# Attention's suffix sums: low parts of the later key chunks added by GpSimd, then multiplied by ones once

## The reference

```python
z = einsum('bqhd,bkhd->bhqk', q, k) * HEAD_DIM ** -0.5 + bias
causal = k_pos[None, :] < q_pos[:, None]
log_1m = where(causal, log_sigmoid(-z), 0.0)              # = -softplus(z)
suffix = cumsum(log_1m, axis=3, reverse=True) - log_1m    # over all later keys
att = where(causal, exp(log_sigmoid(z) + suffix), 0.0)
out = einsum('bhqk,bkhd->bqhd', att, v)
```

## Time and profile before

| what | value |
|---|---|
| median of 3 runs | 1523.05 us |
| the profiled execution | 1527.67 us, its span 1526.1 us |
| TensorE busy | 1472.7 us, 97% of the span |
| VectorE busy | 979.4 us, 64% |
| ScalarE busy | 911.1 us, 60% |
| GpSimd busy | 256.0 us, 17% |
| attention, from the first high part to the last `turn_scores` | 860.0 to 1023.7 |
| HBM traffic | 271.65 MB, 178 GB/s over the span |

### The profile page before, as it was taken

How to read it: one execution, slowest core, us unless ns; L and a number is a source line. 1 busy time by engine, 2 the same in 40 slices (tenths; PEclk the granted TensorE clock), 3 DMA queues, 4 the chain that set the end, 5 groups by cost and what they waited for, 6 DMA issues and landing times.

```text
span 1526.1 us, 28437 instructions
## 1 busy us (share of the span) xinstructions
PE 1472.7 (97%) x11288; PEld 1355.4 (89%) x11288; DVE 979.4 (64%) x1486; ACT 911.1 (60%) x1660; POOL 256.0 (17%) x446
## 2 busy tenths in 40 slices
PE   5999989999999999999999989999999999999998
PEld 3887659999999999999889956678999999999997
DVE  4799965797644887644536346654797654776743
ACT  4699876776643776534435556654776644666633
POOL 1389800000000232100000021110000000222200
PEclk9999999999999999999999999999999999999999
DMA  9887682255554455643337366653255554455553
GB/s 363 310 300 263 264 279 93 69 166 167 176 181 151 141 167 166 196 164 132 127 115 260 106 217 231 222 194 104 68 166 167 166 190 156 138 178 164 190 170 100
DMA packets 71765, 273.76 MB, mean 179 GB/s; under 512 B 8032, under 2 KB 10096, under 8 KB 71120
## 3 DMA queue, kind: packets, MB, share of 16 engines
q1 hardware_dynamic: 65248, 246.44, 47.5%
q0 software_dynamic: 6096, 25.15, 4.9%
q10 hardware_dynamic: 288, 0.35, 0.1%
HBM read 262.80 MB, written 8.85 MB: 178 GB/s over the span
## 4 chain that ended last, share of the span: by engine, by line
PE 84%; DVE 7%; ACT 4%; issue 2%; DMA 1%; SPq 0%; DVEq 0%; ACTq 0%
PE ps L704 62%; PE ps L681 6%; PE ps L937 4%; PE ps L754 2%; DVE w_lo L1633 1%; PE ps L990 1%; PE ps L996 1%; PE ps L973 1%; PE ps L1057 1%; PE ps L1009 1%; DVE y L1934 1%; PE ps L1024 1%; DVE ps L1823 1%; DMA x<-x_in_dram 1%; ACT w_hi L1200 1%
## 5 line engine op out<-in xcount | busy, mean ns | idle before, releaser
L704 PE MATMUL ps<-h_hi,w_hi 128*128 128x288 f32 x1920 | 573.9, 299 | 10.6 <-DVE w_lo L1633 8.3
L704 PE MATMUL ps<-h_lo,w_hi 128*128 128x288 f32 x1920 | 567.5, 296 | 0.0
L704 PE MATMUL ps<-h_hi,w_lo 128*128 128x288 f32 x1920 | 567.3, 295 | 0.0
L1633 DVE TENSOR_TENSOR w_lo<-raw,w_hi 128x1024 fp32r<-128x1024 f32 (+1 forms) x296 | 387.2, 1309 | 231.2 <-ACT w_hi L1200 230.9
L1200 ACT ACTIVATE w_hi<-raw 128x1024 fp32r<-128x1024 f32 (+1 forms) x309 | 346.8, 1124 | 108.4 <-PE ps L704 73.4
L704 PEld LDWEIGHTS ps<-h_hi,w_hi 128*128 128x128 f32 x1920 | 362.3, 189 | 18.7 <-DVE w_lo L1633 11.0
L704 PEld LDWEIGHTS ps<-h_lo,w_hi 128*128 128x128 f32 x1920 | 362.4, 189 | 1.0
L704 PEld LDWEIGHTS ps<-h_hi,w_lo 128*128 128x128 f32 x1920 | 362.1, 189 | 0.0
L704 PE MATMUL ps<-act_hi,w_hi 128*128 128x288 f32 x704 | 208.4, 296 | 0.0
L704 PE MATMUL ps<-act_lo,w_hi 128*128 128x288 f32 x704 | 207.7, 295 | 0.0
L704 PE MATMUL ps<-act_hi,w_lo 128*128 128x288 f32 x704 | 207.0, 294 | 0.0
(11 more groups left out here) (256 smaller groups left out, 2072.6 us busy)
## 6 DMA issues: line engine op xcount, KB each, us to landing
raw<-w_k_dram SPq DMA_DIRECT2D x245, 512.0 KB, 3.5
raw<-w_down_dram SPq DMA_DIRECT2D x64, 704.0 KB, 4.1
ada_w<-w_ada_dram SPq DMA_DIRECT2D x71, 512.0 KB, 6.0
k_page<-cache_kt_dram SPq DMA_DIRECT2D x32, 512.0 KB, 5.1
v_page<-cache_v_dram POOLq DMA_DIRECT2D x32, 512.0 KB, 5.2
ada_h<-w_ada_dram SPq DMA_DIRECT2D x7, 512.0 KB, 6.4
ada_u<-w_ada_dram SPq DMA_DIRECT2D x6, 512.0 KB, 15.9
ada_g<-w_ada_dram SPq DMA_DIRECT2D x6, 512.0 KB, 6.3
```

Source lines behind the costliest of these rows:

```text
L704: mm = pe.matmul(ps[:, BANK[b], 0:HALF], lhsT=w[s][:, kb * P:(kb + 1) * P], rhs=v[:, at, :] if down else v[:, at, lo:hi], start=(at == 0 a ...
L1633: dve.tensor_tensor(w_lo[s][:, 0:cols], raw[n % RING][:, 0:cols], w_hi[s][:, 0:cols].bitcast(F32), ALU.subtract).then_inc(s_lo, 1)
```

## The change

For the low part alone, the chunks are added up before they are multiplied by ones. GpSimd makes, in the new tile `lo_sum[j]` of 3 x 128 columns, chunk 2 + chunk 3 (queries of chunk 3, L2358 of the new file), chunk 1 + chunk 2 (queries of chunk 2, L2360), and chunk 1 + the first sum (queries of chunk 3, L2363), in `low_sums(j, i)`. PE's new `suffix_sums(j, i)` multiplies three unsummed pieces of 128 columns (L1015), waits for `lo_summed`, and multiplies the sums, 128 columns (L1018) and 256 (L1020); `suffix_part` keeps its ones-matmuls for the high part only. `lo_sum` lies behind `w_hi[0]` and `w_hi[1]`, in space that the attention leaves free. In the passes 2 to 7 head 1's triangle matmuls on the low part now stand ahead of `seq_scores`, its ones-matmuls behind it. GpSimd's `low_sums` stand ahead of its wait for banks in pair 0, ahead of `stage_new(sp_st)` in pair 1, and from then on between `stage_new(sp_st)` and the loads of the V pages.

```diff
--- before.py
+++ after.py
@@ -461,6 +461,10 @@
         q_seq = place("q_seq", [P, PAIRS, 4 * TS], at=behind_raw(2))
 
+        lo_sum = [place(f"lo_sum{j}", [P, 3 * P], F32R, at=[w_off + j * FH * P * 4 + C * P * 4, w_off + (j + 1) * FH * P * 4])
+                  for j in range(2)]
+
         s_one, s_two = ((SLOT[O_LOAD] + n) % RING for n in (1, 2))
         k_page += [place(f"k_page{2 + t}", [P, PAIRS * PAGE], at=ring_at(raw_off, (O_LOAD + 2 * t) % RING)) for t in range(2)]
@@ -539,6 +543,7 @@
         z_done, exped, capped, lned, sp_done, suffixed, att_done, av_done = (
             sem(n) for n in ("z_done", "exp_done", "exp_capped", "ln_done", "softplus_done", "suffix_added",
                              "att_done", "av_done"))
+        lo_pair, lo_summed = sem("low_parts_of_two_chunks"), sem("low_parts_summed")
         sp_hi_done, sp_lo_done = sem("softplus_hi"), sem("softplus_lo")
         seq_z_copied, seq_turned, seq_exped, seq_capped, seq_lned, seq_sp = (
@@ -989,15 +994,31 @@
                     at, n = chunk_cols(c)
                     pe.matmul(flat[:, b0 + at:b0 + at + n], lhsT=tri_r[:], rhs=part[:, at:at + n],
                               start=False, stop=True, skip_group_check=True)
+                if low:
+                    return
                 for c in range(3):
                     at = chunk_cols(c)[0]
                     for c2 in range(c + 1, 4):
                         at2, n2 = chunk_cols(c2)
-                        mm = pe.matmul(flat[:, b0 + at + (c2 - c) * P:b0 + at + (c2 - c) * P + n2],
-                                       lhsT=neg_ones_r[:], rhs=part[:, at2:at2 + n2],
-                                       start=False, stop=True, skip_group_check=True)
-                if low:
-                    mm.then_inc(suffixed, 1)
+                        pe.matmul(flat[:, b0 + at + (c2 - c) * P:b0 + at + (c2 - c) * P + n2],
+                                  lhsT=neg_ones_r[:], rhs=part[:, at2:at2 + n2],
+                                  start=False, stop=True, skip_group_check=True)
+            def suffix_sums(j, i):
+
+                b0, low, added = 3 * j * 512, sp_lo[j], lo_sum[j]
+                at = [chunk_cols(c)[0] for c in range(4)]
+                for to, src in ((at[0] + P, low[:, at[1]:at[1] + P]), (at[1] + P, low[:, at[2]:at[2] + P]),
+                                (at[2] + P, low[:, at[3]:at[3] + P])):
+                    pe.matmul(flat[:, b0 + to:b0 + to + P], lhsT=neg_ones_r[:], rhs=src, start=False, stop=True,
+                              skip_group_check=True)
+                pe.wait_ge(lo_summed, 2 * i + j + 1)
+                pe.matmul(flat[:, b0 + at[1] + 2 * P:b0 + at[1] + 3 * P], lhsT=neg_ones_r[:], rhs=added[:, 2 * P:3 * P],
+                          start=False, stop=True, skip_group_check=True)
+                pe.matmul(flat[:, b0 + at[0] + 2 * P:b0 + at[0] + 4 * P], lhsT=neg_ones_r[:], rhs=added[:, 0:2 * P],
+                          start=False, stop=True, skip_group_check=True).then_inc(suffixed, 1)
             def av_pair(i):
                 if i > 0:
@@ -1113,6 +1134,7 @@
                 elif n in (4, 5):
                     suffix_part(n - 4, 0, False)
                     suffix_part(n - 4, 0, True)
+                    suffix_sums(n - 4, 0)
             new_scores()
             z_pair(1)
             new_suffix()
@@ -1123,8 +1145,10 @@
             suffix_part(0, 1, False)
             suffix_part(0, 1, True)
             suffix_part(1, 1, False)
+            suffix_sums(0, 1)
             seq_suffix(0)
             suffix_part(1, 1, True)
+            suffix_sums(1, 1)
             seq_output(0)
             z_pair(2)
             turn_output(0)
@@ -1140,9 +1164,11 @@
                 suffix_part(0, i, False)
                 turn_output(i - 1)
                 suffix_part(0, i, True)
+                suffix_sums(0, i)
                 suffix_part(1, i, False)
+                suffix_part(1, i, True)
                 seq_scores(i)
-                suffix_part(1, i, True)
+                suffix_sums(1, i)
                 turn_scores(i)
                 if i + 1 < PAIRS:
                     z_pair(i + 1)
@@ -2318,6 +2344,27 @@
             pool.memset(sp_st[:], 0.0).then_inc(buffers_free, 1)
             pool.memset(q_seq[:], 0.0).then_inc(buffers_free, 1)
             pool.wait_ge(buffers_free, 4)
+            def low_sums(j, i):
+                low, added = sp_lo[j], lo_sum[j]
+                one, two_, three = 512, 1024, 896
+                pool.wait_ge(sp_lo_done, 2 * i + j + 1)
+                if i:
+                    pool.wait_ge(suffixed, 2 * i + j - 1)
+                    pool.wait_ge(q_staged, 4 * i + 4)
+                    pool.wait_ge(new_staged, 4 * i + 2 if i > 1 else 4)
+                pool.tensor_tensor(added[:, 2 * P:3 * P], low[:, two_ + P:two_ + 2 * P].bitcast(F32),
+                                   low[:, three:three + P].bitcast(F32), ALU.add).then_inc(lo_pair, 1)
+                pool.tensor_tensor(added[:, 0:P], low[:, one + P:one + 2 * P].bitcast(F32),
+                                   low[:, two_:two_ + P].bitcast(F32), ALU.add)
+                pool.wait_ge(lo_pair, 2 * i + j + 1)
+                pool.tensor_tensor(added[:, P:2 * P], low[:, one + 2 * P:one + 3 * P].bitcast(F32),
+                                   added[:, 2 * P:3 * P].bitcast(F32), ALU.add).then_inc(lo_summed, 1)
+            low_sums(0, 0)
+            low_sums(1, 0)
             for b in (O0 - 2, O0 - 1):
                 wait_drained(pool, b)
@@ -2350,8 +2397,16 @@
             for i in range(1, NS):
                 pool.wait_ge(k_used, i)
                 stage_q(i)
+                if i == 1:
+                    low_sums(0, i)
+                    low_sums(1, i)
+                    pool.wait_ge(lo_summed, 2 * i + 2)
                 pool.wait_ge(seq_suffixed, i)
                 stage_new(sp_st, sp_new, i)
+                if i > 1:
+                    low_sums(0, i)
+                    low_sums(1, i)
+                    pool.wait_ge(lo_summed, 2 * i + 2)
                 pool.wait_ge(seq_av, i)
                 for t in range(PAGES):
                     page_load(pool, i, t, v_page, cache_v, v_in)
```

## The result

| | before | after |
|---|---|---|
| median, both on the same chip | 1523.34 us (1522.79 to 1527.38) | 1538.08 us (1534.62 to 1539.20) |
| ratio | | 1.0083, 95% interval 1.0062 to 1.0103 |
| profiled execution, its span | 1527.67, 1526.1 us | 1534.62, 1533.0 us |
| attention, first `z_pair` to the first output block | 175.87 us | 187.84 us |
| of it: `z_pair(0)` to `z_pair(1)` (pair 0) | 31.55 | 35.27 |

The kernel became slower, by 0.8%. The last five lines are differences of start times of TensorE's (PE) first `z_pair` matmul and first output block in the two traces. Attention alone is 12.0 us longer: 3.7 in pair 0, 0.1 in pair 1, 8.2 in the six passes. The spans differ by 6.9 only, because the profiled execution of before had lost some 4.6 us ahead of attention, with a granted clock of 0.95 from 200 to 300 us where the one of after had 1.00.

What follows compares the result with a forecast made beforehand. TensorE, busy 97%, was taken as the bound, each pass hanging on `z_pair`. Passes 7.0, tail 0.2, pair 0 2.2 and pair 1 0.1 gave +9.5 us over the median 1523.05: 1532.5 us, range 1526 to 1540.

Steps and rivals of the forecast that it cites:

- The hold of the first addition: Passes: GpSimd's first addition for head 0 held until VectorE's sp_lo of head 1 ends, lasting about 1.7 us.
- not held: Rival: additions run beside VectorE's sp_lo, 0 a pass, 1522.6 us, about the same; chance 0.12.
- sums in time: Rival: additions end by 978.6, PE never waits, -0.47 a pass, 1519.3 us, faster; chance 0.03.
- One pass, +1.17: Passes 2 to 7: PE's wait and the moved triangle delay head 1's weights by 1.17 us, times 6, +7.0.
- The saving of 0.3 us a head: Ones-matmuls on the low part: five of 768 columns for six of 1280 save 0.3 us a head, 4.8 for 16.
- only the number counts: Low end for the ones-matmuls' saving: 0.12 us a head if only the number of matmuls counted.
- Pair 0, +2.2: Between the Q blocks: PE waits for GpSimd's sums, +2.5, less 0.3 for head 1, +2.2 us.
- Either way the third ends about 865.6: Pair 0: whether one addition or none fits between sp_lo and w_lo, the third ends about 865.6.
- the clock falls: Rival: granted clock falls behind PE's waits, some 1.5 us each; 1541 us if in each pass; chance 0.05.
- Pair 1, +0.1: Pair 1: between a gain of 0.3 and a loss of 1.3 us, taken as +0.1.
- The meeting that it feared: Pair 1: head 1's additions meet VectorE's TENSOR_SCALAR and the chain behind it, and may hold it up; loss up to 1.3.
- V pages, nothing: Passes: loads issued behind the additions stay hidden with 2 us to spare and cost nothing; uncovered, up to 2 us a pass.

Runs made afterwards that it cites:

- Small additions: Changed kernel, with GpSimd's three additions in passes 2 to 7 taking 4 columns in place of 128; 1533.42 us.
- VectorE's order: Changed kernel with V pages issued by SyncE, and VectorE doing seq_o and the first part of pair_o between its two sp_lo; 1534.70 us.
- Pair 0 as it was: Kernel of "V pages from SyncE", with six ones-matmuls again for pair 0, whose additions are made but not read; 1536.02 us, ratio 1.0078.
- Additions that nobody reads: Changed kernel's GpSimd additions and V-page issue kept, but TensorE does the old kernel's matmuls without lo_sum; 1538.57 us, ratio 1.0079.
- Both: Changed kernel, passes 2 to 7 with head 1's high part ahead of head 0's ones-matmuls, V pages issued by SyncE; 1529.32 us, ratio 1.0026.
- Head 1's high part first: Changed kernel, with TensorE taking head 1's high part ahead of head 0's ones-matmuls in passes 2 to 7; 1544.28 us, ratio 1.0131.
- V pages from SyncE: Changed kernel, with V pages issued by SyncE ahead of the K pages, not by GpSimd behind the additions; 1535.07 us, ratio 1.0061.

## Why the prediction was right, and where it was off

Forecast: 1532.5 us (1526 to 1540), slower with 0.85, by 9.5 us. Measured: 1538.08, within the range, slower; 12.0 us in the attention of the traces, 14.7 between the medians (the interval of the ratio is 9.4 to 15.7 us). The 2.7 us between these two aren't explained; the profiled execution of after was the fastest of its four.

- **The hold of the first addition: right.** Forecast, shifted by 3.30: PE goes on at 983.60. Measured 983.58. "Small additions" and "VectorE's order" show the cause. The rival "not held" (0.12) fell by the same rows, and "sums in time" with it.
- **One pass, +1.17: right, measured +1.27.** Head 1's high part came 1.44 later where 1.34 was forecast, since the two matmuls behind the sums took 0.34 (983.58 to 983.92) and not 0.22; `seq_scores` +2.01 (forecast 2.03). `seq_copy` ends last, with `weights` straight behind, as forecast. What the sum lacked is its last step: it puts `weights` 0.63 us behind the start of `seq_copy` (984.71 to 985.34), though the earlier trace rows have 0.69 for `seq_copy` itself; the trace has 0.73 (987.99 to 988.72). With 0.73 the forecast would have been +1.27. Passes 2 to 7 together +8.17 with the tail, against 7.2: 0.24 of it is a wait for a V page, and 1.53 the last pass and its tail (forecast 1.37).
- **The saving of 0.3 us a head: wrong, 0.13.** Of the two ends given, 0.12 for "only the number counts" was the right one: matmuls of 128 columns start 0.11 us apart in a row, and the five are mostly such. The Trainium skill (TensorE: Matmul & The Clock Gate, section Back-to-back issue gap) has 56 ns for an isolated one, by the formula that the prediction cites, and 81 ns in a stream with weight loads; the trace shows 110, and decides. It cost the forecast 0.2 us in all, because head 1's saving wasn't on the path.
- **Pair 0, +2.2: the step that was off most, +3.72.** The mechanism was the forecast one: the second addition held by `w_lo` as well, the third ending behind it. ("Either way the third ends about 865.6" doesn't follow: with one addition in between, its own rates give 865.2. `w_lo`, itself held for 0.25 us, made it 865.5 on that scale.) The sums' part is 2.3, "Pair 0 as it was" takes back all of 3.7, and the rest, some 1.4 us, is the fall of the clock behind the wait: thirteen matmuls at 0.24 us in place of 0.13. The rival "the clock falls" had 0.05 and was priced for every pass; it happened in pair 0 alone, where the wait is the longest. It should have stood as a term there.
- **Pair 1, +0.1: right** (+0.08). The meeting that it feared took place: `att_s` was ready some 0.2 us later behind the two longer VectorE instructions, and the shorter sums behind it took back 0.1 of that.
- **V pages, nothing: right by little.** "Hidden with 2 us to spare" wasn't so. Pages landed up to 9.2 us after issue where 6.9 was taken from the earlier trace rows, because they now run beside the K pages; PE waited once, for 0.24 us. "Additions that nobody reads" shows that the pages alone could have cost all of it. What kept it near zero was the other wait, which the forecast didn't say.
- **The Trainium skill's rule on the port** (SBUF — State Buffer, section Who interferes with whom) was taken in the right direction for the passes. That VectorE can be the one that is held came true in pair 0, where the first addition, started between `sp_lo` and `w_lo`, lengthened `w_lo` from 1.22 to 1.47 us, and in pair 1, where the TENSOR_SCALAR took 0.61 in place of 0.42.

## What to carry to other kernels

Work moved to GpSimd costs what its neighbour on VectorE lets it: look at what VectorE runs from the moment that releases the GpSimd instruction, and if it reads from SBUF (two operands for certain, and in pair 1 here even one), count until its end. Price what is removed by the starts of matmuls of the same width, not by their columns. And what stands on GpSimd's queue behind the added work, here DMA issues, is a second cost, which the first may hide: taking away the first wait made this kernel slower, and only both repairs together brought the old passes back.

## What the runs showed of the hardware

- Instructions on GpSimd and VectorE that read SBUF held each other: an addition of 128x128 took 0.46 us beside casts from PSUM, 1.62 beside a 1.44 us `sp_lo`, and one of 128x4 took 1.37 in place of 0.19. VectorE's `w_lo` of pair 0 took 1.47 or 1.48 us in the traces in which an addition ran into it, and 1.22 in the old kernel. One operand in SBUF was enough in pair 1: a TENSOR_SCALAR took 0.61 in place of 0.42, a COPY 0.47 in place of 0.22, and the addition between them 0.64.
- All six kernels with a PE wait of 2.3 us in pair 0 had the granted clock fall later. In five it fell in the wait or within 2 us of its end and stayed at 1.2 GHz for 3 to 7 us (`z_pair(0)` to `z_pair(1)` 35.3 to 36.4 us); with "Both" it fell some 15 us later. Of the eight waits of 1.6 to 2.2 us for V pages in "Head 1's high part first" and "Additions that nobody reads", six had such a fall in them or within 2 us of their end. Behind attention every one of the twelve traces has a PE wait of 2.30 us for `w_lo`, and ten have the fall there (the earlier trace rows for the old kernel), two don't. Waits of 1.3 us in passes that were otherwise full went by at 1.00. One of 1.6 in pair 1 was followed by a fall in one kernel and not in the others. So the length of a wait alone doesn't decide it.
- Pages of 512 KB that are under way at the same time share the rate. In "V pages from SyncE" the four V pages are issued ahead of the four K pages (in pass 5 from 979.7 to 983.3, and from 988.7 on), and a V page landed after at most 6.5 us. In "Additions that nobody reads" the two groups are issued over each other (in the pass shown from 945.6 and from 946.6 on), and it took up to 11.0.
- Narrow matmuls in a row start 0.11 us apart, narrow ones behind a wide one come closer: the six of the earlier trace rows (384, 256, 128, 256, 128, 128 columns) start 0.23, 0.12, 0.06, 0.17 and 0.06 us apart, and the next matmul 0.11 behind the last.
